# Key search of three heads in layer 0 and two heads in layer 1 done for both latent tiles at once

## The reference, cut to what matters

```python
q = (xb @ p['peer_wq']).reshape(PEER_CHUNK, PEER_HEADS, 2, PEER_KEY_HALF)
s = jnp.einsum('thcd,ckd->thck', q, p['peer_subkeys']).astype(jnp.float32)
sv, si = lax.top_k(s, PEER_TOPK)
...
top_s, pos = lax.top_k(cand_s, PEER_TOPK)
...
u = jnp.take(p['peer_u'], eidx, axis=0)
v = jnp.take(p['peer_v'], eidx, axis=0)
act = jax.nn.gelu(jnp.einsum('ted,td->te', u, xb), approximate=False) * gate
return jnp.einsum('te,ted->td', act, v)
```

## Time and profile before

| | |
|---|---|
| median of 3 runs | 2601.49 us (2597.07 to 2603.72) |
| profiled execution | 2591.99 us |
| span of the profile, first to last instruction | 2590.0 us |
| mean granted TensorE clock | 0.906 of full speed |
| PE matmul busy | 2055.9 us (79%) |
| DVE busy | 1835.6 us (71%) |
| ACT busy | 1145.9 us (44%) |
| POOL busy | 978.4 us (38%) |
| data moved | 980.25 MB, mean 378 GB/s |

### The profile page before, as it was taken

The page is one execution under the profiler, slowest core; times in us unless marked ns, Lnnn a source line. Parts: engine busy times, 40 slices in busy tenths (PEclk is TensorE's granted clock), DMA queues, the critical chain, the costliest instruction groups (busy, mean ns, idle before and its releaser), DMA issues.

```text
span 2590.0 us, 26276 instructions
## 1 busy us (share of the span) xinstructions
PE 2055.9 (79%) x6968; PEld 1088.7 (42%) x6968; DVE 1835.6 (71%) x4200; ACT 1145.9 (44%) x3145; POOL 978.4 (38%) x916
## 2 busy tenths in 40 slices
PE   6997787778979876988677797898877887667766
PEld 2554444544445444444334344444543444333322
DVE  0147996896667779976979556684597787867776
ACT  2123474345247443744443724563244644333333
POOL 1012343333434443554342444341134443344553
PEclk9998888988989988989988999999888998798888
DMA  9588999999999999999999999998699999999997
GB/s 345 174 295 315 403 398 399 404 380 357 415 399 369 390 396 388 402 413 411 413 416 367 356 392 407 394 403 327 242 411 369 407 408 388 414 379 420 421 420 329
DMA packets 215704, 980.25 MB, mean 378 GB/s; under 512 B 17660, under 2 KB 75544, under 8 KB 117272
## 3 DMA queue, kind: packets, MB, share of 16 engines
q0 software_dynamic: 123648, 855.69, 81.4%
q1 hardware_dynamic: 91928, 123.05, 13.8%
HBM read 977.62 MB, written 1.05 MB: 378 GB/s over the span
## 4 chain that ended last, share of the span: by engine, by line
PE 34%; DVE 26%; DMA 20%; ACT 10%; issue 9%; POOL 1%; SPq 0%; POOLq 0%; DVEq 0%; ACTq 0%
DMA EXPERT<-in_peer_uv,FIX 19%; PE VS L1133 13%; PE PA L902 10%; DVE EXPERT L1876 9%; DVE ACC L1886 3%; DVE SCR L1423 2%; PE PA L930 2%; PE PB L826 2%; PE VS L855 1%; ACT L1362 1%; ACT DIAG L1377 1%; ACT WEI L1372 1%; PE PB L1123 1%; DVE SI L1828 1%; DVE SCR L1825 1%
## 5 line engine op out<-in xcount | busy, mean ns | idle before, releaser
L1133 PE MATMUL VS<-EXPERT,DIAG 128*128 128x512 f32 x2304 | 1166.4, 648 | 237.8 <-ACT DIAG L1377 236.1
L734 POOL DMA_INDIRECT EXPERT<-in_peer_uv,FIX x768 | 904.0, 1177 | 1078.1 <-PE VS L1133 733.0
L1876 DVE CUSTOM_DVE_ANT_0 EXPERT<-EXPERT,H 128x1024 f32<-128x1024 f32 x768 | 923.7, 1224 | 305.5 <-DMA EXPERT<-in_peer_uv,FIX 294.9
L1133 PEld LDWEIGHTS VS<-EXPERT,DIAG 128*128 128x128 f32 x2304 | 455.7, 208 | 810.5 <-issue 470.4
L1370 ACT ACTIVATE GEL<-DOT 128x1 f32<-128x1 f32 x768 | 155.1, 202 | 1012.8 <-DVE DOT L1876 987.1
L902 PE MATMUL PA<-WT,HT 128*128 128x512 f32 (+2 forms) x720 | 295.3, 556 | 11.2 <-issue 8.0
L1886 DVE SCALAR_TENSOR_TENSOR ACC<-EXPERT,WEI,ACC 128x1024 f32<-128x1024 f32 x192 | 246.3, 1283 | 30.8 <-ACT WEI L1372 29.6
L1377 ACT ACTIVATE DIAG<-IDN,WEI 128x128 f32<-128x128 f32 x576 | 231.4, 402 | 69.4 <-PE VS L1133 51.5
L1372 ACT ACTIVATE WEI<-GEL,GATE 128x1 f32<-128x1 f32 x768 | 226.4, 295 | 25.0
L1123 PE MATMUL PB<-HT,WT 128*128 128x128 f32 (+1 forms) x1472 | 211.2, 304 | 27.2 <-issue 26.0
L1123 PEld LDWEIGHTS PB<-HT,WT 128*128 128x128 f32 x1472 | 204.9, 216 | 51.2 <-issue 48.7
(11 more groups left out here) (194 smaller groups left out, 1714.4 us busy)
## 6 DMA issues: line engine op xcount, KB each, us to landing
EXPERT<-in_w_ada POOLq DMA_DIRECT2D x48, 1024.0 KB, 13.3
WT<-in_peer_wq SPq DMA_DIRECT2D x92, 512.0 KB
WT<-in_w_in SPq DMA_DIRECT2D x48, 512.0 KB
WT<-in_w_out SPq DMA_DIRECT2D x48, 512.0 KB
EXPERT<-in_peer_uv,FIX POOLq DMA_INDIRECT x768
WT<-in_w_in SPq DMA_DIRECT2D x16, 384.0 KB
WT<-in_w_in SPq DMA_DIRECT2D x16, 288.0 KB
WT<-in_mla_wq_up SPq DMA_DIRECT2D x4, 512.0 KB
```

What stands on the lines that cost most here:

```text
L734: pool.indirect_dma_start(out=EXPERT[:, j, :], out_offset=None, in_=a["peer_uv"], in_offset=bass.IndirectOffsetOnAxis(ap=FIX[:, par, j:j + ...
L1133: ins = nc.tensor.matmul(VSUM[n][:, :], DIAG[:, i, :], EXPERT[:, j, D + n * W:D + (n + 1) * W], start=first, stop=last_one)
L1876: nc.vector.tensor_tensor_reduce(out=EXPERT[:, j, 0:D], in0=EXPERT[:, j, 0:D], in1=H2[:, b % HB, :], scale=1.0, scalar=0.0, op0=ALU.mult, ...
```

## The change

Of the latent tiles, layer 0 now searches heads 0 to 4 for each tile alone and heads 5, 6 and 7 for both at once (before: 0 to 5 alone, 6 and 7 joint). Layer 1 searches heads 0 to 5 alone and heads 6 and 7 jointly (before: none jointly). In layer 1 the first stretch of the weave now ends at slot 96 of block 4 instead of slot 112, and the number of search stages in it is 10 instead of 6. In layer 0 the same formula, which is not changed, gives 14 stages instead of 10.

```diff
-ALONE = {(0, CTX): PH, (0, LAT): 6, (1, LAT): PH}
+ALONE = {(0, CTX): PH, (0, LAT): 5, (1, LAT): 6}
...
-    rest = first[4:] + front(1, LAT, (1,), keys=False) + attention(1, LAT, 1) + outward(1, LAT, (1,)) + picks[:6]
-    plan += weave(plan, rest, stream_of(4, 0, SLOTS - AHEAD))
-    plan += weave(plan, picks[6:], stream_of(4, SLOTS - AHEAD) + [("last", 0)] + stream_of(5, 0, SLOTS - 2 * AHEAD))
+    joint = 2 + 4 * (PH - ALONE[1, LAT])
+    rest = first[4:] + front(1, LAT, (1,), keys=False) + attention(1, LAT, 1) + outward(1, LAT, (1,)) + picks[:joint]
+    plan += weave(plan, rest, stream_of(4, 0, SLOTS - 2 * AHEAD))
+    plan += weave(plan, picks[joint:], stream_of(4, SLOTS - 2 * AHEAD) + [("last", 0)] + stream_of(5, 0, SLOTS - 2 * AHEAD))
```

## The result

The changed kernel takes 2608.18 us (median of 20 runs, 2601.39 to 2615.52), the kernel before on the same chips 2600.18 us (20 runs). The ratio is 1.0029, 95% interval [1.0018, 1.004]: 7.5 us slower by the ratio (8.0 by the medians), where I forecast 11.9 us faster. That lies above my range of 2580 to 2604. By my bound of 0.3% it is just within "the same", but the interval leaves no change out. The profiled execution took 2608.31 us, with a span of 2606.3.

The account below looks back on a forecast made before the run. The prediction took the kernel to be bound by DMA bytes while slots run. Its terms, -9.4 + 3 + 0 - 4 - 1.5 = -11.9 us, gave a median of 2589.6 us, with a range of 2580 to 2604.

Parts of the forecast that it names:

- my bound of 0.3%: Whole run: a measurement can tell about 0.3%, 7.8 us, from no change; faster is below 2593.7, slower above 2609.3.
- layer 1's first stretch: Block 4's slots before 96: denser background, 21.9 units a slot instead of 18.8, costs +3 us; bounds 0 and 19.4.
- layer 0's blocks 2 and 3: Block 2's background grows, block 3's shrinks, and the two shifts cancel: 0 us, bounds -1 and +4.
- the end of block 1: Two searches beside this end go elsewhere, easing a hole of 4.6 us: -1.5 us, bounds -4.6 and +3.
- Weights: Three head loads go, six pieces of 512 KB, 3.15 MB at 3.0 us a MB: -9.4 us.
- What stays in place: Up to slot 111 of block 1, about 960 us, and between the layers, the plan stays the same.
- the bound of 19.4: Upper bound for layer 1's first stretch: 19.4 us if every DVE lag became a hole.
- the 20 I counted on: Gather buffers: eight buffers at 2.53 us a slot cover about 20 us of an engine's delay.
- The end of block 4: After close, the next pick comes behind slot 8 of block 5, removing a 5.0 us hole: -4 us, bounds -5 and +1.
- DVE becomes the bound in block 4: Rival, 8%: in the stretch of 96 slots DVE's lags are not absorbed, costing 19.4 us; +10.0, 2611.5 us.
- The holes move and don't close: Rival, 27%: block ends stay bound by close, memset and restarted buffers whatever search lies there; -6.4, 2595.1 us.

Follow-up runs that it names:

- light_8: Kernel before, but tile 1's eight heads in layer 1 load only a quarter of their query weights, 6.3 MB less; 0.9928 against the kernel before.
- l1_apart_96: Kernel before with only layer 1's first stretch ended at slot 96 of block 4 instead of 112, no joint head there; 1.0026 against the kernel before.
- l0_seven: Kernel before with one joint head (7) in layer 0 instead of two, layer 1 as before; 1.0054 against the kernel before.
- both_seven: Kernel before with one joint head in each layer and block 4's first stretch to slot 100; 1.0033 against the kernel before.
- l0_102: Layer 0's part of the change alone, with its second stretch ended at slot 102 of block 2 instead of 96; 1.0044 against the kernel before.
- l1_joint_112: Layer 1's heads 6 and 7 joint, but the first stretch runs to slot 112 as before, layer 0 as before; 1.0098 against the kernel before.
- close_first: Layer 0's part of the change alone, with attention's first stage moved behind the close of block 1; 1.0030 against the kernel before.
- l0_fill: Layer 0's part alone, with tile 1's output weights held until slot 123 of block 1 is used; 1.0012 against the kernel before.
- hold_8: Changed kernel, but slots 48 to 95 of blocks 2 and 4 look 8 slots ahead for their search, not 16; 1.0015 against the kernel before.
- pick_later: Kernel before with one pick moved from one slot after last to behind slot 7 of block 5; 0.998, 2599.37 against 2602.21 us.
- l1_seven: Kernel before with only head 7 joint in layer 1 and the first stretch to slot 100 of block 4; 0.999 against the kernel before.
- dve_light_l1: Layer 1's part of the change alone, with three wide experts operations in layer 1 replaced by one copy; 0.9979 against the kernel before.

## Why the prediction was wrong

The runs lie 19.4 us above the forecast. Two terms made nearly all of it in about equal parts: layer 1's first stretch (7.7 us off) and layer 0's blocks 2 and 3 with the end of block 1 (8.8 us off). In both the sum asked how dense the background is or how many searches stand at a block's end, and the runs answered to where each stage falls.

- **Weights (-9.4):** right. 86 pieces, 119.90 MB, 13.4% of the DMA engines; the queue's time fell by 8.8 us, and light_8 measured 2.9 us a MB where I took 3.0.
- **What stays in place:** right; slot 112 of block 1 came at 962.3 us, before at 963.5.
- **Layer 1's first stretch (+3):** the first step that failed. I read a price off two stretches, 2% for six units, and took it as linear. The period's idle time rose by 7.7 us (12.7 instead of 5.0), and the gathers' own packets took 344.0 us instead of 341.0 for the same bytes: about +11. Only the bound of 19.4 covered it. That the shorter stretch does it is shown by l1_apart_96; the form of the price is not. Within block 4, 18.0 to 20.2 units a slot idle alike (5.2, 5.0 and 4.9 us) and 21.9 idles 8 to 9 us more. Block 3 at 21.5 units (l0_seven, both_seven) idles 10 to 13 us more than at 20.8. But at 20.8 its slots 0 to 119 already idle some 11 us, at 20.1 (three joint heads) 15, and l0_102 idled with 14.8 and l1_joint_112 31.5 us with 18.8. So what stands at which slot counts as much as the density, and no single threshold fits all of them. I also let each lag be absorbed alone, against a ring of eight full buffers. The two new holes are chains through ACT, PE and DVE in which POOL waits some 10 us, half of the 20 I counted on; that the ring was part empty when they began is my reading, no run shows it.
- **Layer 0, blocks 2 and 3 (0) and the end of block 1 (-1.5):** the second step that failed, wrong in sign. Period 2 idles 5.2 us more on average in the six kernels with three joint heads, nearly all of it in the hole that follows the end of block 1: from slot 120 of block 1 to slot 12 of block 2 they idle 7.0 to 10.4 us, the ten with layer 0 as before 2.2 to 3.3. Period 3 idles 2.1 us more, within its spread, but in the second half of block 3 the eight kernels and the ten don't overlap (4.2 to 6.6 and -1.1 to 3.5 us), which chance would hardly give. I let the two shifts between blocks 2 and 3 cancel, by their densities. With the weights' -3.1 that gives about +4, measured +5.2. I took two searches out of the way of `close` and thought the way free, but attention's first stage stands there now. Moved away (close_first), the first dot product comes 1.4 us sooner after the last, and the runs gain nothing. The hole is not due to the timing of the weights (l0_fill), not to a held slot (hold_8 keeps it, 0.55 in the window) and not to the density of block 2 (l0_102); its cause stays open, and so does that of the holes in block 3, which no run took up.
- **The end of block 4 (-4):** the mechanism was right. The hole is gone; the period's idle time fell by 2.2 us, where I took 4, and by 3.8 in pick_later.
- **The rivals:** "DVE becomes the bound in block 4" came nearest in time, 2611.5 us, and in its place, and it named the held slot. Its sign came too: the window from 2140 to 2160 us, between slots 80 and 96, has a DMA share of 0.87 with DVE busy for 19.86 of 20 us. But by the timelines DVE is not what begins it: in the second hole DVE first idles 10.09 us for PE, and is full only afterwards; in the first it is 66% busy. With lighter DVE work the loss left the runs and not the profile, so DVE's share is neither shown nor excluded. "The holes move and don't close" holds for block 1 alone.

The terms as measured: -8.8 for the weights, +10.7 in block 4, +5.2 in period 2, +2.1 in period 3 and -2.2 in period 5 make +7.0; the runs gave +7.5 [4.7, 10.4]. That they agree so well is partly luck, since each comes from single profiles with a spread of several us.

## What to carry to other kernels

When a kernel is bound by bytes and an engine's lag is hidden by a ring of buffers, don't price denser background by a slope between two stretches: here block 4 idled alike from 18.0 to 20.2 units a slot and 8 to 9 us more at 21.9, while other stretches idled at 14.8 and 18.8. Taking loads away by merging work also changes where every later stage falls; look at what stands at each block's end and beside which slots, since that decided more here than the bytes. l1_seven, which merges one head in layer 1 and stays at 20.2, and pick_later, which only moves one stage, are at or just under the kernel before; no kernel here that computes everything beats it by more than 0.2%.

## What the runs showed that I had not expected

In block 4 the gathers' packets took 343.6 to 344.6 us in the five kernels with two joint heads (l1_joint_112 and dve_light_l1 too) and 340.2 to 341.9 in nine with layer 1 as before, for the same 138.8 to 139.9 MB; no run here says why. And one execution's period 3 can be 11.6 us longer than another's with an identical plan, with the same bytes: the difference of a change of 0.3% can't be read from two profiles, only its places can.
